# A relative-bias table stored once and read with rows shifted by one, and a delta-rule head whose instructions stand in another order

## The chip, the cores and the metric

One Trainium2 chip, one of its cores. The metric is the device time of one execution of the whole program, in microseconds (us); shorter is better.

## What is computed

Two blocks of two layers each, on 256 positions of width 1024, all in float32. The first block's layer is a feed-forward part (SwiGLU), a hybrid mixer, and a second feed-forward part. The second block's layer is a mixer with four branches and a feed-forward part. The change touches two places: the chunked delta rule of the first block's mixer, and the relative-position bias of one attention branch of the second block.

```python
# first block, mixer: for each of 8 heads and each chunk
g = cumsum(g)                                   # log decays
decay = exp(where(lower_incl, g_i - g_j, -inf))
lmat  = where(strict, (k_beta @ k.T) * decay, 0)
sol   = triangular_solve(lmat + I, [v * beta, k_beta * exp(g)])
attn_intra = (q @ k.T) * decay
...                                             # a scan over chunks gives o_a
merged = sigmoid(gate_a) * (o_a @ w_branch_a) + sigmoid(gate_b) * (o_b @ w_branch_b)
...
# second block, branch A: scores get a bias by distance
rel_idx = clip(query - key, -128, 128) + 128
scores  = q @ k.T * d**-0.5 + rel_table[:, rel_idx]
```

## The kernel before

Every weight matrix is cut into units of 128 x 2048 elements (1 MB). SyncE loads a unit into one of three slots (`load_unit`, line 242); ScalarE rounds it to a high part (`split_hi`, L248), VectorE takes the low part by subtraction (`split_lo`, L254), and TensorE multiplies with both (`product3`, L262 to L264, three matmuls for one product). A product over one unit (`feature_product`) is 48 such matmuls of 256 columns. The next load into a slot waits until the slot's unit has been split. The order of work on every engine is written out by hand; the engines meet at counting semaphores, and an engine that waits holds up all that stands behind the wait in its own list.

**The bias table.** During the first feed-forward part of layer 0, `setup_act` (L428 to L437) stores the table of relative biases to a DRAM tensor `bias_rows`: its 8 rows (2 layers x 4 heads) of 384 numbers are each written 128 times (L436), on ScalarE's DMA queue. Both layers of the second block read it back (L1532) with a row stride of 383, so that partition s gets the row that begins at 128 - s. `scores_a` (L1546) adds it to the scores by a matmul with the identity. GpSimd masks one corner (L2062).

**The mixer and its delta head.** `mix1_pe`, `mix1_act`, `mix1_dve` and `mix1_pool` first go through 28 input units (`N1`), numbered 0 to 27. The result of a "q", "k", "v" or "z" unit passes a SiLU that is made of four ScalarE operations (L809, L811, L813, L855), one VectorE operation (L916) and one GpSimd operation (L1427), one unit behind the products. The last unit, 27, is "v" heads 6 and 7. Behind the input units comes the delta head, for four groups of two heads and two chunks (`GROUPS`, the buffers `Ab`, `Mb`, `Lb`, `Ub`, `Tb`):

- TensorE (`mix1_delta_pe`): for each group four matmuls that spread the decays (`g_rows`, L1165) and four of k with k (`kk`, L1169); then for each group k with q (`qk`, L1176), which waits for `x_abs` and `glast_kept` of the group; the product of the first gate unit (28, `pair_gate_pe(0)`); a gather of the 16 x 16 diagonal blocks (L1182), which waits for the last `m_ready` and the first `attn_done`; the branch unit 29; the gate unit 30; the scatter of the inverted blocks (L1193); the branch unit 31; a product with the identity (L1200); and then three levels that merge the blocks (L1206, L1211, L1217).
- ScalarE (`mix1_delta_act`): for each group exponentials of the decays (L1279), absolute differences (L1283), the decay (L1286) and a small exponential (L1288) that waits for VectorE's `glast_kept`. Then the split of unit 31, three operations of the gate's sigmoid (L888, L890, L892), the copy of the gathered blocks (L1292) and the sigmoid's last operation (L896).
- VectorE (`mix1_delta_dve`): `glast_kept` (L1356), then L = kk x beta x decay for each group (L1364), the split of unit 31, the attention of each group (L1371), the gate's minimum (L984), and the solution of all 16 x 16 blocks, 14 dependent steps (`blocks_dve`, L1332 to L1342) with a spread behind it (L1346).
- GpSimd (`mix1_pool`): masks of the decay (L1430) and of L (L1436, it signals `m_ready`), then the decayed q (L1442).

Of the kernel before, what the change touches and what calls it, by code (L numbers as in the profile page):

```python
# [34 lines left out]
ARENA = 19712  # L35
# [45 lines left out]
def constants_2():  # L81
# [7 lines left out]
    for n in range(64, 80):  # L89
# [6 lines left out]
             "turn": turn, "freq": freq}  # L96
# [11 lines left out]
def hybrid_stack_kernel(nc, d, out):  # L108
    ctx = ExitStack()
    with ctx:  # L110
# [46 lines left out]
        bias_rows = nc.dram_tensor("bias_rows", [DEPTH, 4, P, 384], F32, kind="Internal").ap()  # L157
# [270 lines left out]
        def setup_act(e):  # L428
# [7 lines left out]
            e.dma_start(bias_rows.rearrange("l h s m -> (l h) s m"), ext.unsqueeze(1).to_broadcast([DEPTH * 4, P, 384]))\  # L436
             .then_inc(stored, 16)  # L437
# [232 lines left out]
        def b4(i):  # L670
            return bank[i][:].rearrange("p (i n) -> p i n", i=4)
# [66 lines left out]
        def pair_gate_pe(e, l, r0, u0, n):  # L738
            if n < 2:
                e.wait_ge(*V["l_done"](l, 2 * n))  # L740
            elif n < 4:
                e.wait_ge(*V["od_r"](l, 2 * n - 4))
            else:
                e.wait_ge(*V["p_scaled"](l, n - 2))
            feature_product(e, unit(r0, u0 + N1 + 2 * n), gate_bank(n), xhi, xlo)

        def pair_branch_pe(e, l, r0, u0, n):
            if n < 2:
                e.wait_ge(*V["l_done"](l, 2 * n + 1))
            elif n < 4:  # L750
                e.wait_ge(*V["od_r"](l, 2 * n - 3))
            if n == 0:
                e.wait_ge(*V["o_lo"](l, HEADS - 1))
# [31 lines left out]

        def mix1_act(e, l, r0, u0, j):
# [6 lines left out]
            for n in range(N1 + TAIL):  # L793
# [7 lines left out]
                if n - 1 in SILU:  # L801
                    m = SILU.index(n - 1)
                    if n - 1 in CONV:
                        e.wait_ge(*V["tap"](l, CONV.index(n - 1) * 4 + 3))
                    else:
                        e.wait_ge(*V["kept"](l, PLAIN.index(n - 1)))
                    if m >= 2:
                        e.wait_ge(*V["silu"](l, m - 2))
                    e.activation(sg[m % 2], home(n - 1), ACT.Abs).then_inc(V["s_abs"].sem, 1)  # L809
                    e.wait_ge(*V["s_abs"](l, m))  # L810
                    e.activation(sg[m % 2], sg[m % 2], ACT.Exp, scale=-1.0).then_inc(V["s_exp"].sem, 1)  # L811
                    e.wait_ge(*V["s_exp"](l, m))
                    e.activation(sg[m % 2], sg[m % 2], ACT.Ln, bias=one).then_inc(V["s_ln"].sem, 1)  # L813
# [38 lines left out]
                if n - 1 in SILU:  # L852
                    m = SILU.index(n - 1)
                    e.wait_ge(*V["s_min"](l, m))
                    e.activation(sg[m % 2], sg[m % 2], ACT.Exp).then_inc(V["s_sigmoid"].sem, 1)  # L855
# [48 lines left out]
        def mix1_dve(e, l, r0, u0, j):  # L904
# [3 lines left out]
            for n in range(N1 + TAIL):  # L908
# [4 lines left out]
                if n - 1 in SILU:  # L913
# [1403 lines left out]
```

## Time and profile before

| what | value |
|---|---|
| median of 3 runs | 2628.71 us (2627.85 to 2634.68) |
| profiled execution, its own time | 2631.52 us |
| its span, first to last instruction | 2629.8 us |
| TensorE matmul busy | 2460.1 us (94% of the span) |
| VectorE busy | 1531.4 us (58%) |
| ScalarE busy | 1380.6 us (52%) |
| GpSimd busy | 177.5 us (7%) |
| mean granted TensorE clock | 0.975 of full speed |
| weights and the rest read from HBM | 382.95 MB, 147 GB/s over the span |

The profiled execution's time is 1.7 us over its span and 2.8 us over the median. PE is TensorE, DVE VectorE, ACT ScalarE, POOL GpSimd, SP SyncE; L262 is line 262 of the kernel. A granted clock of 1.0 is 2.4 GHz and one of 0.5 is 1.2 GHz. Busy TensorE time includes matmuls at the lower clock, so that the share of 94% does not say that nothing can be gained there. A row of a window view has, in this order: the stretch, its length, the busy us (and instructions) of PE, PE's weight loads, DVE, ACT and POOL, the granted clock, the mean busy share of the core's 16 DMA engines, and GB/s.

### The profile page before, as it was taken

To read this page: it belongs to the slowest core of one execution; us is meant where nothing else is said; L and a number is where in the kernel's file an instruction comes from. 1 tells how busy PE (TensorE), PEld (TensorE's weight loads), DVE (VectorE), ACT (ScalarE), POOL (GpSimd) and SP (SyncE) were. 2 spreads that over 40 slices of the span, in tenths; PEclk is the share of its full clock that TensorE was granted. 3 is DMA by queue.
4 is the path that set the end of the run, shared out by engine and by line. 5 is a ranking of instruction groups with operands and counts; after the bars stand their busy time and mean duration, and the time that the engine had idled before them with its cause. 6 is when DMAs were issued, how large, how long until landed. Compare 5 with 4: busy or idle time off the path is not lost.

```text
span 2629.8 us, 42657 instructions
## 1 busy us (share of the span) xinstructions
PE 2460.1 (94%) x17457; PEld 2291.8 (87%) x17457; DVE 1531.4 (58%) x1826; ACT 1380.6 (52%) x1828; POOL 177.5 (7%) x197
## 2 busy tenths in 40 slices
PE   7996998899999999999899899999889999997998
PEld 7995988898998998898799899888879988896897
DVE  5554667555555555566655555566475555757554
ACT  5553777255544554678535555445644444555443
POOL 0000112100000000011200000000030000003000
PEclk9998999899999999999899999999989999998999
DMA  6555444125455455444314455543345554334453
GB/s 216 183 182 130 145 135 138 36 81 189 146 190 177 158 191 167 149 134 129 97 49 146 146 188 191 168 135 112 121 130 177 183 185 144 113 113 160 144 184 128
DMA packets 313127, 387.38 MB, mean 147 GB/s; under 512 B 10780, under 2 KB 288296, under 8 KB 313000
## 3 DMA queue, kind: packets, MB, share of 16 engines
q1 hardware_dynamic: 311704, 383.94, 45.7%
q10 hardware_dynamic: 1296, 1.66, 0.5%
q8 instruction: 91, 1.49, 0.2%
q14 instruction: 36, 0.29, 0.0%
HBM read 382.95 MB, written 2.62 MB: 147 GB/s over the span
## 4 chain that ended last, share of the span: by engine, by line
PE 74%; DVE 10%; ACT 9%; issue 4%; DMA 2%; POOL 0%; SPq 0%; DVEq 0%; ACTq 0%; POOLq 0%
PE bank L262 22%; PE bank L263 21%; PE bank L264 21%; DVE wlo L254 4%; ACT whi L248 4%; DVE arena L952 1%; DMA raw<-in_w_in 1%; PE bank L1211 1%; PE bank L1206 1%; PE bank L348 1%; PE bank L722 1%; DVE arena L1976 1%; ACT arena L1875 1%; ACT arena L314 1%; PE bank L1217 1%
## 5 line engine op out<-in xcount | busy, mean ns | idle before, releaser
L254 DVE TENSOR_TENSOR wlo<-raw,whi 128x2048 fp32r<-128x2048 f32 x360 | 830.3, 2307 | 525.6 <-ACT whi L248 524.6
L262 PE MATMUL bank<-xhi,whi 128*128 128x256 f32 x3712 | 1065.2, 287 | 12.1 <-DVE arena L550 6.8
L263 PE MATMUL bank<-xlo,whi 128*128 128x256 f32 x3712 | 1053.3, 284 | 0.0
L264 PE MATMUL bank<-xhi,wlo 128*128 128x256 f32 x3712 | 1053.1, 284 | 0.0
L248 ACT ACTIVATE whi<-raw 128x2048 fp32r<-128x2048 f32 x360 | 682.1, 1904 | 154.9 <-PE bank L264 133.7
L262 PEld LDWEIGHTS bank<-xhi,whi 128*128 128x128 f32 x3712 | 715.4, 193 | 23.0 <-issue 17.1
L263 PEld LDWEIGHTS bank<-xlo,whi 128*128 128x128 f32 x3712 | 715.2, 193 | 4.9 <-issue 1.9
L264 PEld LDWEIGHTS bank<-xhi,wlo 128*128 128x128 f32 x3712 | 714.9, 193 | 0.0
L262 PE MATMUL bank<-whi,yhi 128*128 128x512 f32 x608 | 238.0, 391 | 9.2 <-ACT yhi L472 6.2
L263 PE MATMUL bank<-wlo,yhi 128*128 128x512 f32 x608 | 237.4, 390 | 0.0
L264 PE MATMUL bank<-whi,ylo 128*128 128x512 f32 x608 | 236.6, 389 | 0.0
L262 PEld LDWEIGHTS bank<-whi,yhi 128*128 128x128 f32 x608 | 114.4, 188 | 33.2 <-ACT yhi L472 7.8
L264 PEld LDWEIGHTS bank<-whi,ylo 128*128 128x128 f32 x608 | 114.2, 188 | 24.6
L263 PEld LDWEIGHTS bank<-wlo,yhi 128*128 128x128 f32 x608 | 114.4, 188 | 20.9
L262 PE MATMUL bank<-yhi,whi 128*128 128x256 f32 x384 | 112.9, 294 | 13.8 <-DVE ylo L2009 12.5
L262 PE MATMUL bank<-whi,xhi 128*128 128x256 f32 (+1 forms) x320 | 107.0, 334 | 16.1 <-DVE arena L2051 11.2
L472 ACT ACTIVATE yhi<-arena 128x512 fp32r<-128x512 f32 x44 | 27.8, 632 | 167.5 <-PE bank L264 154.9
L263 PE MATMUL bank<-ylo,whi 128*128 128x256 f32 x384 | 111.7, 291 | 0.0
L264 PE MATMUL bank<-yhi,wlo 128*128 128x256 f32 x384 | 111.6, 291 | 0.0
L263 PE MATMUL bank<-wlo,xhi 128*128 128x256 f32 (+1 forms) x320 | 105.7, 330 | 0.0
L264 PE MATMUL bank<-whi,xlo 128*128 128x256 f32 (+1 forms) x320 | 105.6, 330 | 0.0
L1427 POOL TENSOR_TENSOR arena<-arena 128x512 f32<-128x512 f32 x32 | 42.4, 1324 | 931.4 <-ACT arena L855 931.4
(377 smaller groups left out, 2867.4 us busy)
## 6 DMA issues: line engine op xcount, KB each, us to landing
raw<-in_w_in SPq DMA_DIRECT2D x92, 1024.0 KB, 5.2
raw<-in_ffn_w_in SPq DMA_DIRECT2D x88, 1024.0 KB, 5.1
raw<-in_ffn_w_out SPq DMA_DIRECT2D x44, 1024.0 KB, 4.9
raw<-in_w_gate SPq DMA_DIRECT2D x32, 1024.0 KB, 5.4
raw<-in_w_up SPq DMA_DIRECT2D x32, 1024.0 KB, 5.5
raw<-in_w_down SPq DMA_DIRECT2D x32, 1024.0 KB, 5.0
raw<-in_w_branch_b SPq DMA_DIRECT2D x8, 1024.0 KB, 5.0
raw<-in_w_branch_a SPq DMA_DIRECT2D x8, 1024.0 KB, 5.0
```

The lines of the kernel that those rows point to most:

```text
L248: e.activation(whi[s][:], raw[s][:], ACT.Copy).then_inc(hi_done[s], 1)
L254: e.tensor_tensor(wlo[s][:], raw[s][:], whi[s][:].bitcast(F32), ALU.subtract).then_inc(lo_done[s], 1)
L262: e.matmul(o, ahi, bhi, start=start, stop=False, skip_group_check=True)
L263: e.matmul(o, ahi, blo, start=False, stop=False, skip_group_check=True)
L264: return e.matmul(o, alo, bhi, start=False, stop=stop, skip_group_check=True)
L314: e.activation(xn[:, t, :], x[:, t, :], ACT.Square, accum_out=sumsq[:, t:t + 1]).then_inc(sumsq_done, 1)
L348: mm = e.transpose(tp[c // 2][:, c % 2, t * P:(t + 1) * P], xn[:, t, c * P:(c + 1) * P], ident)
L472: e.activation(hhi.rearrange("p c t -> p (c t)"), hbuf, ACT.Copy).then_inc(hhi_done, 1)
L722: e.matmul(bank[2 + m % 2][:], ones, sqr[m % 2], start=True, stop=True).then_inc(V["square_sum"].sem, 1)
L952: ins = e.scalar_tensor_tensor(o, src, w, o, ALU.mult, ALU.add)
L1206: mm = e.matmul(b4(g)[:, i, :], Lb[g][:, i, :], Ub[g][:, i, :], start=True, stop=True)
L1427: e.tensor_tensor(home(n - 1), home(n - 1), sg[m % 2], ALU.mult).then_inc(V["silu"].sem, 1)
```

## The change

The bias table is now written once, 8 rows of 384 numbers. It is read with a row stride of one (`bias_by_row`), so that partition s gets the row that begins at 1 + s, which is the old partition 127 - s. The matmul that adds it uses an anti-identity (`flip`, one more constant of 128 columns in the second table) in place of the identity, and the masked corner is in partitions 0 to 63.

In the delta head nothing is added and nothing left out; the instructions stand in another order on TensorE, ScalarE, VectorE and GpSimd, and some waits are placed elsewhere.

```diff
-        bias_rows = nc.dram_tensor("bias_rows", [DEPTH, 4, P, 384], F32, kind="Internal").ap()
+        bias_rows = nc.dram_tensor("bias_rows", [DEPTH * 4, 384], F32, kind="Internal")
+        def bias_by_row(l):
+            return bass.AP(tensor=bias_rows, offset=l * 4 * 384 + 1, ap=[[1, P], [384, 4], [1, T]])
...
-            e.dma_start(bias_rows.rearrange("l h s m -> (l h) s m"), ext.unsqueeze(1).to_broadcast([DEPTH * 4, P, 384]))\
-             .then_inc(stored, 16)
+            e.dma_start(bias_rows.ap(), ext).then_inc(stored, 16)
...
-            e.dma_start(bias_a, bias_rows[l].rearrange("h s m -> h (s m)")[:, P:P + P * 383]
-                        .rearrange("h (s m) -> s h m", m=383)[:, :, 0:T]).then_inc(small_in, 16)
+            e.dma_start(bias_a, bias_by_row(l)).then_inc(small_in, 16)
...
-            e.matmul(o[:, 0:128], bias_a[:, h, 0:P], ident, start=False, stop=True, skip_group_check=True)
+            e.matmul(o[:, 0:128], bias_a[:, h, 0:P], flip, start=False, stop=True, skip_group_check=True)
...
+        KK_ORDER = (1, 2, 3, 0)
+        def place(g):
+            return KK_ORDER.index(g)
         def mix1_delta_pe(e, l, r0, u0):
             e.wait_ge(*V["o_lo"](l, HEADS - 1))
-            e.wait_ge(*V["normed"](l, len(NORM) - 1))
-            e.wait_ge(*V["pre_copied"](l, len(CONV) - 1))
-            for g in range(GROUPS):
+            for g in range(GROUPS):
+                if g < 2:
+                    e.wait_ge(*V["pre_copied"](l, len(CONV) - 2 + g))
                 for i in range(4):
                     mm = e.matmul(b4(g)[:, i, :], tile_col(gg, g, i).to_broadcast([P, P]), le, start=True, stop=True)
                 mm.then_inc(V["g_rows"].sem, 1)
-                for i in range(4):
-                    h, t = 2 * g + i // 2, i % 2 * P
-                    mm = e.matmul(b4(4 + g)[:, i, :], kT[:, h, t:t + P], kT[:, h, t:t + P], start=True, stop=True)
-                mm.then_inc(V["kk"].sem, 1)
+            pair_gate_pe(e, l, r0, u0, 0)
+            e.wait_ge(*V["normed"](l, len(NORM) - 1))
+            for g in KK_ORDER[:3]:
+                kk_pe(e, g)
             for g in range(GROUPS):
...
                 mm.then_inc(V["qk"].sem, 1)
-            pair_gate_pe(e, l, r0, u0, 0)
+            e.wait_ge(*V["p_min"](l, 0))
+            kk_pe(e, 0)
+            pair_branch_pe(e, l, r0, u0, 0)
             e.wait_ge(*V["m_ready"](l, GROUPS - 1))
             e.wait_ge(*V["attn_done"](l, 0))
...
             mm.then_inc(V["gathered"].sem, 1)
-            pair_branch_pe(e, l, r0, u0, 0)
             pair_gate_pe(e, l, r0, u0, 1)
+            pair_branch_pe(e, l, r0, u0, 1)
             for b in range(4):
...
                 mm.then_inc(V["scattered"].sem, 1)
-            pair_branch_pe(e, l, r0, u0, 1)
...
         def mix1_delta_act(e, l, r0, u0):
...
+            pair_gate_act(e, l, r0, u0, 0)
             split_hi(e, unit(r0, u0 + N1 + 3))
-            pair_gate_act(e, l, r0, u0, 0)
+            pair_sigmoid_act(e, l, 0)
+            silu_log_act(e, l, N1 - 1)
+            silu_exp_act(e, l, N1 - 1)
             e.wait_ge(*V["gathered"](l))
             e.activation(small_l, bank[0][:, 0:256], ACT.Copy).then_inc(V["l_compact"].sem, 1)
-            pair_sigmoid_act(e, l, 0)
...
-            for g in range(GROUPS):
-                e.wait_ge(*V["kk"](l, g))
+            for g in KK_ORDER:
+                if g == 0:
+                    silu_min_dve(e, l, N1 - 1)
+                e.wait_ge(*V["kk"](l, place(g)))
...
                 up.then_inc(V["l_done"].sem, 1)
+                if g == 1:
+                    pair_min_dve(e, l, 0)
+                if g == 3:
+                    attn_dve(e, l, range(3))
+            attn_dve(e, l, range(3, 4))
             split_lo(e, unit(r0, u0 + N1 + 3))
-            for g in range(GROUPS):
-                e.wait_ge(*V["a_mask"](l, g))
-                e.wait_ge(*V["qk"](l, g))
-                e.tensor_tensor(flat(Ab[g]), bank[g][:], flat(Ab[g]), ALU.mult).then_inc(V["attn_done"].sem, 1)
-            pair_min_dve(e, l, 0)
             blocks_dve(e, l)
```

`silu_log_act`, `silu_exp_act`, `silu_min_dve` and `silu_pool` are the SiLU of a unit as functions; for unit 27 they are called in the delta head. `kk_pe` and `attn_dve` are the loops that stood in place. GpSimd masks L in the order 1, 2, 3, 0 and multiplies unit 27's SiLU behind that. The spread in `blocks_dve` waits for that SiLU as well.

How the lists move is seen at three places. On **TensorE**, in the delta head of layer 0, before. The names are buffers: `table,small` spreads the decays, `arena 128x128` is kk or qk, `xhi,whi` opens a gate product, `yhi,whi` a branch product, and `128x16` is the gather.

```order
L1165 MATMUL bank<-table,small 128x128 x4
L1169 MATMUL bank<-arena 128x128 x4
...
L1176 MATMUL bank<-arena 128x128 x16
L262 MATMUL bank<-xhi,whi 128x256
...
L1182 MATMUL bank<-table,arena 128x16 x16
L262 MATMUL bank<-yhi,whi 128x256
...
L1193 MATMUL bank<-table,arena 128x128 x16
L262 MATMUL bank<-yhi,whi 128x256
```

And the same place after the change, where L1190 is the spread of the decays, L1175 kk, L1201 qk, L1209 the gather, L1220 the scatter and L1226 the product with the identity:

```order
L1190 MATMUL bank<-table,small 128x128 x16
...
L268 MATMUL bank<-xhi,wlo 128x256
L1175 MATMUL bank<-arena 128x128 x12
L1201 MATMUL bank<-arena 128x128 x16
L1175 MATMUL bank<-arena 128x128 x4
L266 MATMUL bank<-yhi,whi 128x256
...
L1209 MATMUL bank<-table,arena 128x16 x16
L266 MATMUL bank<-xhi,whi 128x256
...
L1220 MATMUL bank<-table,arena 128x128 x16
L1226 MATMUL bank<-table,arena 128x128 x16
```

The first gate product moved ahead of kk and qk, the first branch product ahead of the gather, and both products of the second pair stand between gather and scatter; nothing stands between scatter and the product with the identity.

On **VectorE**, from the last input unit's split to the blocks, before:

```order
L254 TENSOR_TENSOR wlo<-raw,whi 128x2048
L916 SCALAR_TENSOR_TENSOR arena<-arena 128x512
L1356 TENSOR_TENSOR small<-bank,small 128x1 x8
L1364 SCALAR_TENSOR_TENSOR arena<-bank,small,arena 128x128 x16
L254 TENSOR_TENSOR wlo<-raw,whi 128x2048
L1371 TENSOR_TENSOR arena<-bank,arena 128x512 x4
L984 SCALAR_TENSOR_TENSOR pre<-bank,pre 128x2x256
L1332 TENSOR_TENSOR arena<-table,arena 128x256
```

and after, with L1391 for `glast_kept`, L1401 for L, L998 for the gate's minimum, L1360 for the attention and L809 for the SiLU's minimum:

```order
L258 TENSOR_TENSOR wlo<-raw,whi 128x2048
L1391 TENSOR_TENSOR small<-bank,small 128x1 x8
L1401 SCALAR_TENSOR_TENSOR arena<-bank,small,arena 128x128 x4
L998 SCALAR_TENSOR_TENSOR pre<-bank,pre 128x2x256
L1401 SCALAR_TENSOR_TENSOR arena<-bank,small,arena 128x128 x8
L1360 TENSOR_TENSOR arena<-bank,arena 128x512 x3
L809 SCALAR_TENSOR_TENSOR arena<-arena 128x512
L1401 SCALAR_TENSOR_TENSOR arena<-bank,small,arena 128x128 x4
L1360 TENSOR_TENSOR arena<-bank,arena 128x512
L258 TENSOR_TENSOR wlo<-raw,whi 128x2048
L1366 TENSOR_TENSOR arena<-table,arena 128x256
```

The gate's minimum stands behind the first group's L, and the SiLU's minimum and the split of unit 31 came down past three groups.

On **ScalarE**, behind the last of the four groups, after the change (L905, L907, L909 and L913 are the gate's sigmoid, L795 to L804 the SiLU of unit 27, L1321 the copy of the gathered blocks):

```order
L1314 ACTIVATE small<-small 128x2
L905 ACTIVATE pre<-bank 128x2x256
L907 ACTIVATE pre<-pre 128x2x256
L909 ACTIVATE pre<-pre,const_cols 128x2x256
L252 ACTIVATE whi<-raw 128x2048
L913 ACTIVATE pre<-pre 128x2x256
L795 ACTIVATE arena<-arena 128x512
L797 ACTIVATE arena<-arena 128x512
L799 ACTIVATE arena<-arena,const_cols 128x512
L804 ACTIVATE arena<-arena 128x512
L1321 ACTIVATE arena<-bank 128x256
```

The SiLU of unit 27 stood ahead of the four groups before; now it stands behind the gate's sigmoid.

## Rows read from the trace of the kernel before

**Rows 1.** The page's chain that ended last, shares of the span by engine
```profile
PE 74%; DVE 10%; ACT 9%; issue 4%; DMA 2%; POOL 0%; SPq 0%; DVEq 0%; ACTq 0%; POOLq 0%
```

**Rows 2.** TensorE's waits over the whole span: us in total, times, longest
```profile
PE bank L1176 <- DVE small L1356: 10.5, 8, 2.3
...
PE bank L1182 <- DVE arena L1371: 10.2, 2, 5.1
...
PE bank L1165 <- ACT pre L825: 4.8, 2, 2.4
```

**Rows 3.** Windows of the same work in layer 0 and in layer 1 (columns as told above)
```profile
187.18:234.16 46.98, 24.38 (x150) 21.75 (x149) 16.54 (x16) 17.58 (x24) 0.00 (x0) 0.79 0.63 144
...
1027.93:1057.43 29.50, 24.38 (x150) 21.75 (x149) 16.54 (x16) 13.78 (x19) 0.00 (x0) 0.94 0.55 176
```

**Rows 4.** ScalarE in order of time, layer 0: start, us, instruction, [idle before, releaser]
```profile
189.22 0.80 ACTq L436 DMA_DIRECT2D bias_rows<-arena  x1
...
223.70 1.91 ACT L248 ACTIVATE whi<-raw 128x2048 fp32r<-128x2048 f32 x1 [17.77 <-DMA raw<-in_w_in]
```

**Rows 5.** The chain of waits at that place, and the page's loads of the same kind
```profile
195.35 28.33 DMA raw<-in_w_in
...
raw<-in_w_in SPq DMA_DIRECT2D x92, 1024.0 KB, 5.2
```

**Rows 6.** Window in which only the bias write is under way
```profile
214.00:216.00 2.00, 0.00 (x0) 0.00 (x0) 0.00 (x0) 0.00 (x0) 0.00 (x0) 0.54 0.52 79
```

**Rows 7.** Windows, layer 0's delta head, and its last product before L1200
```profile
444.92:506.24 61.32, 48.56 (x354) 47.78 (x354) 33.21 (x80) 27.61 (x56) 15.53 (x14) 0.89 0.22 69
...
500.40:506.24 5.84, 5.84 (x52) 5.84 (x51) 0.65 (x2) 2.92 (x3) 0.00 (x0) 1.00 0.20 64
```

**Rows 8.** Windows of the two stretches at half the clock in it
```profile
463.70:466.80 3.10, 3.10 (x16) 3.10 (x16) 3.10 (x14) 0.00 (x0) 3.10 (x3) 0.51 0.00 0
...
477.40:487.20 9.80, 9.80 (x47) 9.80 (x47) 4.13 (x15) 0.91 (x2) 0.00 (x0) 0.50 0.33 107
```

**Rows 9.** ScalarE in order of time, layer 0's delta head
```profile
447.99 1.89 ACT L248 ACTIVATE whi<-raw 128x2048 fp32r<-128x2048 f32 x1
...
455.09 0.42 ACT L1279 ACTIVATE arena<-bank 128x128 f32<-128x128 f32 x2
...
457.21 0.42 ACT L1279 ACTIVATE arena<-bank 128x128 f32<-128x128 f32 x2
...
473.71 0.58 ACT L888 ACTIVATE pre<-bank 128x512 f32<-128x512 f32 x1
...
474.99 0.72 ACT L892 ACTIVATE pre<-pre,const_cols 128x512 f32<-128x512 f32 x1
```

**Rows 10.** VectorE in order of time, layer 0's delta head
```profile
451.63 2.29 DVE L254 TENSOR_TENSOR wlo<-raw,whi 128x2048 fp32r<-128x2048 f32 x1
...
463.17 4.23 DVE L1364 SCALAR_TENSOR_TENSOR arena<-bank,small,arena 128x128 f32<-128x128 f32 x16
...
476.05 2.48 DVE L1371 TENSOR_TENSOR arena<-bank,arena 128x512 f32<-128x512 f32 x4
...
484.42 0.43 DVE L1332 TENSOR_TENSOR arena<-table,arena 128x256 f32<-128x256 f32 x1 [5.29 <-ACT arena L1292]
...
491.49 2.50 DVE L1346 TENSOR_TENSOR arena<-arena,table 128x512 f32<-128x512 f32 x4
```

**Rows 11.** GpSimd in order of time, layer 0's delta head
```profile
464.86 5.03 POOL L1436 TENSOR_TENSOR arena<-arena,table 128x512 f32<-128x512 f32 x4
```

**Rows 12.** The chain of waits: the gather, and 16 matmuls at full clock
```profile
476.88 7.08 PE bank L1182 x32
...
497.07 3.57 PE bank L1193 x32
```

**Rows 13.** DMA issues: count, KB each, us to landing
```profile
arena<-bias_rows SPq DMA_DIRECT2D x2, 512.0 KB, 6.6
...
arena<-in_g_final SPq DMA_DIRECT2D x1, 512.0 KB, 3.7
```

More of the change, by code:

```diff
@@ L738, in pair_gate_pe @@
         def pair_gate_pe(e, l, r0, u0, n):
-            if n < 2:
-                e.wait_ge(*V["l_done"](l, 2 * n))
-            elif n < 4:
+            if n == 1:
+                e.wait_ge(*V["l_done"](l, place(2)))
+            elif 2 <= n < 4:
                 e.wait_ge(*V["od_r"](l, 2 * n - 4))
-            else:
+            elif n >= 4:
                 e.wait_ge(*V["p_scaled"](l, n - 2))
@@ L748, in pair_branch_pe @@
             if n < 2:
[L749 removed]
+                e.wait_ge(*V["l_done"](l, place(2 * n + 1)))
             elif n < 4:
                 e.wait_ge(*V["od_r"](l, 2 * n - 3))
[L752 to L753 removed]
             if n == 4:
@@ L784, in home, with silu_log_act, silu_exp_act, silu_min_dve @@
             return HOME[KINDS.index(kind)][:, 2 * g:2 * g + 2, :].rearrange("p h t -> p (h t)")
+        def silu_log_act(e, l, n):
+            m = SILU.index(n)
+            if n in CONV:
+                e.wait_ge(*V["tap"](l, CONV.index(n) * 4 + 3))
+            else:
+                e.wait_ge(*V["kept"](l, PLAIN.index(n)))
+            if m >= 2:
+                e.wait_ge(*V["silu"](l, m - 2))
+            e.activation(sg[m % 2], home(n), ACT.Abs).then_inc(V["s_abs"].sem, 1)
+            e.wait_ge(*V["s_abs"](l, m))
+            e.activation(sg[m % 2], sg[m % 2], ACT.Exp, scale=-1.0).then_inc(V["s_exp"].sem, 1)
+            e.wait_ge(*V["s_exp"](l, m))
+            e.activation(sg[m % 2], sg[m % 2], ACT.Ln, bias=one).then_inc(V["s_ln"].sem, 1)
+        def silu_exp_act(e, l, n):
+            m = SILU.index(n)
+            e.wait_ge(*V["s_min"](l, m))
+            e.activation(sg[m % 2], sg[m % 2], ACT.Exp).then_inc(V["s_sigmoid"].sem, 1)
+        def silu_min_dve(e, l, n):
+            m = SILU.index(n)
+            e.wait_ge(*V["s_ln"](l, m))
+            e.scalar_tensor_tensor(sg[m % 2], home(n), 0.0, sg[m % 2], ALU.min, ALU.subtract).then_inc(V["s_min"].sem, 1)
+        def silu_pool(e, l, n):
+            m = SILU.index(n)
+            e.wait_ge(*V["s_sigmoid"](l, m))
+            e.tensor_tensor(home(n), home(n), sg[m % 2], ALU.mult).then_inc(V["silu"].sem, 1)
         def mix1_act(e, l, r0, u0, j):
@@ L800, in mix1_act @@
                     stick_softplus_act(e, l, head_at(n, 1))
[L801 to L813, printed above, removed]
+                if n - 1 in SILU and n < N1:
+                    silu_log_act(e, l, n - 1)
                 if head_at(n, 3) is not None:
@@ L1326, in mix1_delta_act, with attn_dve @@
                 e.activation(flat(Tb[g]), flat(Tb[g]), ACT.Exp, scale=-0.5).then_inc(V["od_r"].sem, 1)
+        def attn_dve(e, l, which):
+            for g in which:
+                e.wait_ge(*V["a_mask"](l, g))
+                e.wait_ge(*V["qk"](l, g))
+                e.tensor_tensor(flat(Ab[g]), bank[g][:], flat(Ab[g]), ALU.mult).then_inc(V["attn_done"].sem, 1)
         def blocks_dve(e, l):
@@ L1431, in mix1_pool @@
                  .then_inc(V["a_mask"].sem, 1)
-            for g in range(GROUPS):
-                e.wait_ge(*V["l_done"](l, g))
+            for g in KK_ORDER:
+                e.wait_ge(*V["l_done"](l, place(g)))
                 e.wait_ge(*V["a_mask"](l, g))
```

40 lines of the change are left out of this document (20 added, 20 removed).

## The prediction, made before the change was run

> **What bounds the kernel now.** First the page's chain of work that ended last: three quarters of it is TensorE [rows 1]. So time is gained only where TensorE waits or runs at the lower clock. Next TensorE's waits. Three of them lie in the delta head, in both layers: 2.4 us for the last unit's copy, 5.3 us ahead of the four qk groups, 5.1 us ahead of the gather; 12.8 us in each layer [rows 2]. Third, windows of the same work in the two layers, from VectorE's last operation on block 9 of the first feed-forward part to the mixer's first normalised chunk. TensorE is busy 24.38 us in both, yet layer 0 takes 46.98 us and layer 1 takes 29.50 us [rows 3]: 17.5 us that only layer 0 pays. Fourth, the granted clock in the delta head: 0.89 on average over 61.32 us [rows 7], and two stretches of 3.1 and 9.8 us at the 1.2 GHz level [rows 8].
>
> **Part 1: the bias table.** The write of the old table, 1536 KB, is issued at 189.22 us. After it ScalarE waits 17.77 us for a load of weights, until 223.70 us [rows 4]. The load had been issued at 195.35 and landed 28.33 us later, where its kind takes 5.2 us [rows 5]. In 214 to 216 us, where TensorE, VectorE and ScalarE all stand still, half of the DMA engines are busy and move 79 GB/s [rows 6]: the write, which the load shares its engines with. The new write has one 128th of the bytes. The load then lands at about 200.6 us; ScalarE wants it at 205.9 (223.70 less 17.77). So 5 us of cover remain, and layer 0 costs here what layer 1 costs, which has no such write: **-17.5 us** [rows 3].
>
> The Trainium skill speaks against this part (DMA: Bandwidth & Descriptors, Specifications): its fabric ceiling of 435 GB/s would move 1.57 MB in 3.6 us, an estimate from that page. By it the write would be over long before the load is wanted, and part 1 would be worth nothing. The row at 79 GB/s decides; what the rule gives is the third rival.
>
> Reading is unchanged in size: 512 KB, 6.6 us to landing [rows 13]. That 128 partitions now read over the same few KB has a neighbour in the trace: the final gain, 512 KB read from one row of 4 KB, lands in 3.7 us [rows 13]. I price it at nothing; its cover is the four input units that are multiplied before the table is needed. The matmul with the other constant has the same shape. The constant adds 64 KB to one load that is issued two units ahead: nothing.
>
> **Part 2: the delta head.** I take layer 0's times; layer 1's waits are the same. The end that counts is the product with the identity (L1200), which starts at 506.24. A product over one unit takes 5.8 us [rows 7], 16 square matmuls 3.6 us at full clock [rows 12], four of them 0.9. Step by step, with TensorE:
>
> 1. It frees at 444.9. The first group's spread of decays needs no wait any more, but the second group's still needs the copy at 447.2: 1.5 us of the 2.4 us wait stays. The spreads end at 450.0.
> 2. The gate product, which stood behind qk, follows: to 455.8. Three groups of kk: to 458.5.
> 3. ScalarE. The SiLU of unit 27 no longer stands ahead of the groups, so they begin when the split at 447.99 ends, at 449.8 instead of 455.09 [rows 9]. Group 0 waits for VectorE, whose split ends at 453.9 [rows 10], until 454.1. The next three follow at the pitch of 2.12 us (457.21 less 455.09), to 460.6. That hides the stalls between qk groups; qk runs through to 462.1.
> 4. The gate's three operations take 2.0 us (473.71 to 475.71 [rows 9]), to 462.7, and its minimum on VectorE 0.7, to 463.4. TensorE waits 1.3 us for it (new wait), then kk of group 0 to 464.4 and the branch product to 470.2.
> 5. On VectorE two groups of L at 1.06 (4.23 over 4), three attentions at 0.62 (2.48 over 4) [rows 10], the SiLU's minimum at 0.7 and L of group 0 end at 469.1; ScalarE's SiLU, behind a split of 1.9, delivers at 467.2, in time. GpSimd's last mask takes 1.26 (5.03 over 4 [rows 11]), to 470.4. The gather starts at 470.5, not 476.88. The split of unit 31 comes down past all this and ends at 471.9; its product needs it at 479.8.
> 6. The gather is 32 array operations of 7.08 us, all at half clock [rows 8, 12]. At full clock I take 3.6 us, since as many operations of the scatter take 3.57 [rows 12]; it is the same number of weight loads. The two ends are 3.6 and 7.1. It ends at 474.1.
> 7. Two products: to 485.6. Under them the blocks, 7.07 us from 484.42 to 491.49, and the spread of 2.5 [rows 10] end on VectorE at 484.1, 1.5 us before they are wanted. The spread also waits for unit 27's SiLU, which GpSimd has done by 471.8. Scatter to 489.2.
> 8. The last copy of the scatter's result on ScalarE was hidden by a branch product; now TensorE waits 0.7 us for it. VectorE's share (a scaling, a split of 2.3, a minimum and two copies behind the spread) ends at 489.0, only just in time.
>
> L1200 starts at 489.9: **-16.3 us in each layer**. As a cross-check, waits fall from 12.8 to 3.8 (1.5, 1.3, 0.3, 0.7), which is 9.0; the clock gives back up to 11% of 61.3, which is 6.7 [rows 7]. That is 15.7, and 0.6 of rounding at the joints. Behind L1200 the order is unchanged and the loads have been issued earlier, not later.
>
> The sum is 17.5 + 2 x 16.3 = 50.1 us off the profiled execution's 2631.5: 2581.4. That execution lies 2.8 over the median of the runs, so I give 2578.6, rounded to **2579 us**.
>
> **The clock, and what I do not know.** The clock fell at 463.7 behind a stretch whose waits were all short, the longest 2.4 us, and at 477.4 behind 5.1 us of waiting. It did not come back in the gather (476.88 to 483.96 [rows 12]) but only under the branch product behind it, at 487.2 [rows 8]. [...] The Trainium skill (TensorE: Matmul & The Clock Gate, "Why this matters for your kernels") names idle gaps as what takes the clock down. By that the gather would cost nothing more; the first fall speaks against reading it so narrowly.
>
> **Rivals.**
> - *The clock falls again* in or behind the gather. For: it stayed low through the gather. Against: it is granted in full through all the later levels with their small matmuls, and the gather is now half as long. Price from 1 to 7.3 us a layer (16.3 less 9.0, all of the clock's share): 2581 to 2593 us.
> - *The wait moves to VectorE or GpSimd.* Steps 5, 7 and 8 have covers of 0 to 1.5 us. Each late us costs one: about 2 a layer, 2583 us.
> - *The write is worth nothing*, since the load is late for another reason. Against it speaks layer 1. 2628.7 less 32.6 is 2596 us.
> - *Slower than before:* 128 rows from one spot of DRAM are read one after the other. The write moved 79 GB/s on eight engines, 10 on each; a read that falls to one engine's 10 GB/s takes 52 us in place of 6.6, 45 more in each layer. Less the 50 gained that is 2628.7 + 91 - 50 = 2670 us. It decides from 25 us more per read on. The final gain's 3.7 us speaks against it.
> - *The order changes nothing*, as the head is bound by its chain of data on all engines, and only the write counts: 2611 us. The 5 us that ScalarE's groups come forward speak against it.
>
> **How the numbers follow.** Chances: my forecast 0.62, the clock 0.2, the moved wait 0.1, the write worth nothing 0.02, only the write 0.03, slower 0.02, and 0.01 that nothing is seen. The range goes from 2574 (2 us in each layer for the roundings of eight steps) to 2592 (nearly all of the clock's share lost in both layers). A difference under 0.3%, some 8 us, can't be told from none. Faster 0.97, same 0.01, slower 0.02.
>
> **What would show it.** Layer 0's window from rows 3 at about 29.5 us, and no load of 28 us in the chain. The delta head from the last input product to the product with the identity at 45 us in place of 61.3, with waits of TensorE of about 4 us; the wait for p_min above 1 us and one of 0.7 ahead of L1226. The gather at 3.6 us. A gather of 7 us, or a clock of 0.5 behind it, is the first rival; a wait on VectorE or GpSimd ahead of the gather or scatter the second. I am wrong as a whole if layer 0 still waits for that load, or if the product with the identity comes less than 9 us earlier.

## The result, and the profile after

The change runs in 2593.07 us (median of 4, 2591.27 to 2595.65), beside 2630.2 us for the kernel before on the same chip (2627.85 to 2634.68): a ratio of 0.9858, 95% interval 0.9841 to 0.9875. That is 37 us faster where 50 were forecast, and 1 us above the top of the range. The profiled execution took 2591.27 us (span 2589.5, mean clock 0.98).

The page of the change, its chain that ended last, by engine:

```profile
PE 75%; DVE 10%; ACT 9%; issue 4%; DMA 0%; POOL 0%; SPq 0%; DVEq 0%; ACTq 0%; POOLq 0%
```

The 2% of DMA of [rows 1] are gone. The waits of TensorE, the ones that answer to [rows 2] (total us, times, longest):

```profile
PE bank L1190 <- ACT pre L844: 2.8, 2, 1.4
...
PE bank L1175 <- DVE pre L998: 2.3, 2, 1.1
...
PE bank L1226 <- ACT arena L1326: 1.6, 2, 0.8
```

L1190 is the spread of the decays, L1175 kk and L1226 the product with the identity. The gather (L1209) is not in the list. It waits 0.3 us a layer for GpSimd's last mask, as the first row of weight loads below shows; before, it waited 5.1 us.

Windows of the change: layer 0's stretch of [rows 3], the whole delta head (from the last input product to L1226, as in [rows 7]), the gather, the stretch from the fall of the clock into the gate product, and the gate product:

```profile
186.02:215.50 29.48, 24.36 (x150) 21.73 (x149) 16.44 (x16) 17.64 (x24) 0.00 (x0) 0.93 0.54 178
425.39:475.21 49.82, 46.40 (x354) 45.66 (x352) 34.03 (x80) 25.27 (x55) 19.47 (x14) 0.93 0.26 85
450.79:457.90 7.11, 7.11 (x33) 7.11 (x34) 2.09 (x1) 0.00 (x0) 6.00 (x5) 0.73 0.45 147
454.00:461.60 7.60, 7.60 (x39) 7.60 (x40) 2.80 (x13) 2.18 (x2) 2.79 (x5) 0.55 0.42 137
457.74:465.09 7.35, 7.35 (x51) 7.35 (x52) 5.81 (x28) 2.18 (x2) 0.00 (x0) 0.79 0.00 0
```

Layer 0's stretch is now as long as layer 1's was: 17.5 us are gone. The head takes 49.8 us in place of 61.3; 45.0 were forecast. In it the gather takes 7.1 us again, and the gate product behind it 7.35 us, at a mean clock of 0.79; with the full clock it takes 6.0 (e4 below).

ScalarE of the change where the write is issued. It needs 0.28 us, and the splits follow with no wait for a load (in [rows 4] ScalarE waited 17.77 us):

```profile
188.12 0.28 ACTq L440 DMA_DIRECT2D bias_rows<-arena  x1
...
202.93 3.71 ACT L252 ACTIVATE whi<-raw 128x2048 fp32r<-128x2048 f32 x2
```

The change's DMA issues answer to [rows 13]. The read of overlapping rows costs what the old one did:

```profile
arena<-bias_rows SPq DMA_DIRECT2D x2, 512.0 KB, 6.6
arena<-in_g_final SPq DMA_DIRECT2D x1, 512.0 KB, 3.6
```

The chain of waits through the end of the head (start us, us, what), where [rows 12] stood before:

```profile
449.44 1.30 POOL arena L1471
450.79 7.12 PE bank L1209 x32
457.90 0.40 PE bank L266
...
470.86 3.59 PE bank L1220 x32
474.46 0.61 ACT arena L1326
475.21 3.81 PE bank L1226 x32
```

Gather, scatter and product with the identity are 32 array operations each; the first takes twice as long as the others. Its weight loads, in the change and for comparison L1226's (count, busy us, mean ns, idle before):

```profile
L1209 PEld LDWEIGHTS bank<-table,arena 128*128 128x128 f32 x64 | 14.0, 310 | 0.6 <-POOL arena L1471 0.6
...
L1226 PEld LDWEIGHTS bank<-table,arena 128*128 128x128 f32 x64 | 7.3, 192 | 1.9 <-issue 1.9
```

A weight load of the gather takes 310 ns where a 128 x 128 load of L1226, at the full clock, takes 192 ns. The gather's weights are `M_blocks[:, :, c]`, every 16th float32 of a row of 2048, a step of 64 bytes. That set the theories for the experiments. **A**: the step makes the gather slow, and the clock falls in or behind it because each of its matmuls multiplies only 16 columns (its moving operand). **B**: the gather is slow because the clock falls in it, as I had read it in the kernel before.

### The profile page after: what moved, and what is told of

Its sections match the earlier page's. It is cut to its first block, busy times and chain, and to the rows that moved or that the text cites. A ratio compares the mean times of both kernels' runs of the same rounds, so it can differ in the third digit from the quotient of the medians.

```text
span 2589.5 us, 42657 instructions
## 1 busy us (share of the span) xinstructions
PE 2457.9 (95%) x17457; PEld 2289.9 (88%) x17457; DVE 1532.7 (59%) x1826; ACT 1380.5 (53%) x1828; POOL 185.5 (7%) x197
## 4 chain that ended last, share of the span: by engine, by line
PE 75%; DVE 10%; ACT 9%; issue 4%; DMA 0%; POOL 0%; SPq 0%; DVEq 0%; ACTq 0%; POOLq 0%
PE bank L266 22%; PE bank L267 21%; PE bank L268 21%; DVE wlo L258 4%; ACT whi L252 4%; DVE arena L966 1%; PE bank L1237 1%; PE bank L1232 1%; PE bank L352 1%; PE bank L725 1%; DVE arena L2011 1%; ACT arena L1910 1%; ACT arena L318 1%; PE bank L1243 1%; PE bank L1209 1%
```

## The experiments

### The two parts alone

```diff
 # e1_bias_only: the kernel before, with
+            e.dma_start(bias_rows.ap(), ext).then_inc(stored, 16)
+            e.dma_start(bias_a, bias_by_row(l)).then_inc(small_in, 16)
 # (and flip, and the other masked corner); head and all else as before
 # e2_head_only: the change, with
-            e.dma_start(bias_rows.ap(), ext).then_inc(stored, 16)
+            e.dma_start(bias_rows.rearrange("l h s m -> (l h) s m"), ext.unsqueeze(1).to_broadcast([DEPTH * 4, P, 384]))\
+             .then_inc(stored, 16)
 # (and the old read, ident, the old corner)
```

> The kernel before with the bias table of the change alone (written once, read with a stride of one row element, anti-identity); the delta head stands as before. If the write of 1.5 MB was what held the load back: layer 0's window from VectorE's last operation on block 9 to the first normalised chunk falls from 47.0 to about 29.5 us and the time falls by 17 to 19 us, to about 2612; the delta head stays at 61.3 us. Rival (the load was late for another reason): the window stays near 47 us and the time near 2630.

> The changed kernel with the old bias table put back; the delta head in its new order. If the two parts add: the time falls by what is left of the change's 37 us, 19 to 22 us, to about 2609, the head from the last input product to the product with the identity takes 49.8 us in both layers as in the change, and layer 0 keeps its wait of 17.8 us for the load. Rival (the parts share something, for instance the phase of the clock): the two parts' gains sum to less than 33 or to more than 41 us.

Measured: the table alone 2612.95 us (2611.49 to 2614.1), ratio 0.9938 [0.9922, 0.9955]; the head alone 2610.25 us (2606.98 to 2611.16), 0.9926 [0.9909, 0.9942]; beside them the kernel before took 2629.61. So 16.7 and 19.4 us, together 36.0, where both at once brought 37. The parts add, within 1.1 us. The table is worth what was forecast, within 1 us. The head is worth 19 in place of 33: that is where the shortfall lies. In the profile of the head alone, the head takes 49.9 us in both layers, as in the change within 0.1.

In the profile of the table alone, the stretch of [rows 3] is as short as in the change:

```profile
186.02:215.50 29.48, 24.33 (x151) 21.72 (x151) 16.45 (x16) 18.09 (x24) 0.00 (x0) 0.95 0.56 178
```

### The gather: the step of its weights, and its width

```diff
 # e3_gather_unstrided
-  mm = e.matmul(bank[0][:, c * BLK:(c + 1) * BLK], M_blocks[:, :, c], const("row_of"), start=True, stop=True)
+  mm = e.matmul(bank[0][:, c * BLK:(c + 1) * BLK], arena[:, 10240 + c * P:10240 + (c + 1) * P], const("row_of"), start=True, stop=True)
 # e4_gather_wide
-  mm = e.matmul(bank[0][:, c * BLK:(c + 1) * BLK], M_blocks[:, :, c], const("row_of"), start=True, stop=True)
+  mm = e.matmul(bank[0][:, c % 4 * P:(c % 4 + 1) * P], M_blocks[:, :, c], ident, start=True, stop=True)
```

> The changed kernel, but the 16 matmuls of the gather take 128 neighbouring columns as weights in place of every sixteenth one; the blocks that it solves are therefore not those of L. Theory (the weights' stride of 16 elements makes the weight loads slow): the gather falls from 7.1 to 3.6 us at the full clock, each layer gains 3.5 us and perhaps the 1.5 us of the clock behind it as well: 7 to 10 us below the change. Rival 1 (128x16 matmuls are slow because they are narrow): the gather stays at 7.1 us and the time at that of the change. Rival 2 (it was the clock alone): the same, 7.1 us.

> The changed kernel, but the gather multiplies with the identity of 128 columns in place of 16 columns, with the same strided weights; what it writes is not the blocks of L. Theory (weights' stride sets the gather's 7.1 us; its few columns take the clock down): the gather still takes 7.1 us, the granted clock stays at 1.0 through it and through the gate product behind it, which falls from 7.35 to 5.9 us: 1.5 us a layer, about 3 us below the change. Rival (the clock falls for the slow weight loads or for the waits ahead, whatever the columns): the clock falls again at the same place and the time is that of the change within 1 us.

Neither gathers the diagonal blocks: the first multiplies neighbouring columns in place of them, the second transposes slices with the identity. Measured: 2585.5 us (2583.26 to 2587.68) and 2590.99 us (2590.46 to 2595.35). The gather in the chain of waits, first without the step, then with it and 128 columns:

```profile
450.49 4.17 PE bank L1209 x32
```

```profile
450.90 7.25 PE bank L1209 x32
```

In the first, part of the gather ran at the half clock (mean 0.87).

Windows of the second, the gather and the gate product behind it:

```profile
450.90:458.16 7.26, 7.26 (x34) 7.26 (x35) 2.09 (x1) 0.00 (x0) 5.98 (x5) 1.00 0.46 144
457.91:463.91 6.00, 6.00 (x52) 6.00 (x52) 4.58 (x22) 2.18 (x2) 0.00 (x0) 1.00 0.00 0
```

Here the clock is at its full 2.4 GHz all through and the gather still takes 7.26 us. That excludes theory B: without any fall of the clock the step gives the whole length. The gather's loads take the same in the change, where the clock falls at 454.0 in the middle of it, as here at the full clock. First the change, then this run:

```profile
L1209 PEld LDWEIGHTS bank<-table,arena x64: 291/310/312, 450.8 to 1269.8; 128*128 128x128 f32 x64
```

```profile
L1209 PEld LDWEIGHTS bank<-table,arena x64: 291/312/313, 450.9 to 1267.0; 128*128 128x128 f32 x64
```

The three numbers are the smallest, median and largest ns. What happens to the clock goes with the width: with 16 columns it falls in or behind the gather, with 128 it holds, and the gate product takes 6.0 us. The profiles of all runs in the new order agree. In the 3 us behind the gather the granted clock is 0.50 to 0.58 in all 13 layers with 16 columns, and 1.00 in all 7 with 128.

### The same computation with another layout

The masked L is written so that the gather finds the weights of one column side by side. GpSimd writes with the step in place of TensorE reading with it:

```diff
 # e5_gather_layout
-        M_blocks = arena[:, 10240:12288].rearrange("p (b c) -> p b c", c=BLK)
+        M_columns = arena[:, 16384:18432].rearrange("p (c b) -> p c b", c=BLK)
...
-                e.tensor_tensor(Mb[g], Lb[g], const("below").unsqueeze(1).to_broadcast([P, 4, P]), ALU.mult)\
+                o = M_columns[:, :, g * 32:g * 32 + 32].rearrange("p c (i k) -> p i k c", i=4)
+                e.tensor_tensor(o, src, below, ALU.mult).then_inc(V["m_ready"].sem, 1)
...
-                mm = e.matmul(bank[0][:, c * BLK:(c + 1) * BLK], M_blocks[:, :, c], const("row_of"), start=True, stop=True)
+                mm = e.matmul(bank[0][:, c * BLK:(c + 1) * BLK], M_columns[:, c, :], const("row_of"), start=True, stop=True)
 # e6_layout_wide: as e5, and the 16 columns eight times
+                mm = e.matmul(bank[0][:, c * BLK:c * BLK + P], M_columns[:, c, :],
+                              const("row_of").unsqueeze(1).to_broadcast([P, P // BLK, BLK]), start=True, stop=True)
```

> The changed kernel, with GpSimd writing its masked L column by column (stride 128) into the free buffers behind it, so that each of the gather's 16 matmuls reads 128 neighbouring weights; nothing is left out. Theory: the gather takes 3.6 us in place of 7.1, and since its 16 columns still take the clock down, the product behind it stays slow for some 3 us: the time of the run with neighbouring weights, about 2586, 7 us below the change. If GpSimd's strided writes are slower than its 1.27 us for a group, the last of them delays the gather by as much, up to 1 us a layer. Rival (the earlier run gained by something else than the stride): within 2 us of the change.

> As the one before, and each matmul of the gather multiplies with its 16 columns repeated eight times (128 columns, of which the next matmul overwrites all but the first 16). Nothing is left out. Theory (width holds the clock, stride sets the length; the two are independent): the gather takes 3.6 us, the granted clock stays at 1.0 through it and behind it, the product behind it takes 5.9 us, and the head from the last input product to the product with the identity takes 49.8 less 3.5 less 1.5, about 45 us, which is what the prediction had: about 2583, 10 us below the change. Rival (the clock also falls for the short waits ahead of the gather): as the one before, about 2586.

> The change itself again, for a second profile. Theory on the 1.5 us that each layer gave back behind the head (a fall of the clock at the 2.4 us wait ahead of the output product, which the kernel before also has, without the fall): the fall comes and goes from one execution to the next, so this profile has it in some of the four output products of the first block's layers and not in the same ones. Rival (the new order causes it): both layers have it again. The time is 2593 within 3 us either way.

Measured, beside 2630.08 us for the kernel before: the layout 2585.91 us (2584.5 to 2587.01), 0.9832 [0.9818, 0.9845]; the layout with 128 columns 2589.29 us (2587.62 to 2591.47), 0.9846 [0.9833, 0.986]; the change again 2591.89 us (2589.46 to 2593.45), 0.9853 [0.9838, 0.9868]. The layout is the fastest version found that does the whole computation (e8 below, at 2587.07 us, is too near to tell apart), and no run of it was as slow as the fastest of the change. GpSimd's mask takes no longer for that: 1.31 us in place of 1.30. The second profile of the change was to settle whether a fall of the clock that both layers have at the 2.4 us wait ahead of the output product, and that the kernel before has not, comes and goes. It does not: both layers have it again, so it comes with the new order. The windows behind that wait, layers 0 and 1:

```profile
603.20:606.30 3.10, 3.10 (x8) 2.42 (x8) 3.01 (x4) 1.47 (x1) 0.00 (x0) 0.50 0.72 252
1415.50:1418.50 3.00, 3.00 (x8) 2.32 (x9) 2.91 (x4) 1.62 (x1) 0.00 (x0) 0.50 0.81 284
```

In the chain of the layout version:

```profile
450.61 1.31 POOL arena L1474
451.97 3.75 PE bank L1209 x32
...
468.82 3.59 PE bank L1220 x32
472.43 0.61 ACT arena L1326
...
473.17 3.81 PE bank L1226 x32
```

The four heads side by side, the row of each from its own profile: the change's 49.82 stands above. With the step and 128 columns (e4):

```profile
425.49:474.02 48.53, 45.09 (x353) 44.34 (x352) 33.88 (x80) 25.25 (x55) 19.45 (x14) 1.00 0.24 77
```

without it and with 16 columns (e5):

```profile
426.57:473.17 46.60, 43.17 (x352) 42.42 (x352) 34.99 (x80) 25.25 (x55) 19.66 (x14) 0.96 0.26 84
```

and without it, with 128 columns (e10, the second profile of e6's kernel):

```profile
427.12:472.44 45.32, 41.67 (x353) 40.90 (x351) 34.96 (x80) 25.46 (x55) 19.71 (x14) 1.00 0.23 74
```

The step costs 3.2 us at either width (49.82 less 46.60, 48.53 less 45.32), the narrow columns 1.3 us with either layout. Without both the head takes 45.3 us; the forecast was 45.0.

### Why the shortest head does not give the shortest kernel

That last version has the shortest head and takes 3.4 us more than the layout with 16 columns. I cut each profile at the ten additions of rows that end each part, and give the length of each stretch:

| us | layer 0: FFN, then mixer | FFN | FFN | layer 1: mixer | FFN | 2nd block: mixer | FFN | mixer | FFN |
|---|---|---|---|---|---|---|---|---|---|
| before | 227.85, 424.86 | 199.38 | 199.03 | 424.15 | 199.40 | 281.25 | 191.18 | 280.83 | 188.54 |
| change | 209.27, 414.03 | 199.20 | 199.03 | 414.13 | 199.19 | 281.12 | 191.17 | 280.59 | 188.59 |
| e5, layout | 207.72, 413.61 | 199.25 | 199.03 | 410.91 | 199.15 | 281.09 | 191.17 | 280.56 | 188.59 |
| e6, layout, wide | 207.74, 409.66 | 200.98 | 201.43 | 409.87 | 200.97 | 281.10 | 191.06 | 282.67 | 188.77 |

FFN is a feed-forward part. The code of the feed-forward parts and of the second block is the same in all. Yet in e6 two of the feed-forward parts take 1.7 and 1.8 us more than in e5 and one 2.4, and a mixer of the second block 2.1. So I asked whether that is chance, or follows from the head:

```diff
 # e8_wide_in_first: as e6, and
+                if l:
+                    mm = e.matmul(bank[0][:, c * BLK:(c + 1) * BLK], M_columns[:, c, :], const("row_of"), start=True, stop=True)
+                    continue
 # e9_layout_again is e5, e10_layout_wide_again is e6
```

> The gather reads neighbouring weights in both layers, and multiplies 128 columns in layer 0 and 16 in layer 1. Between the adds of rows at the end of layer 0's mixer and at the end of the next one (numbers 1 and 3 of ten), the version with 128 columns in both layers took 402.4 us, with 16 in both 398.3 us; layer 0's mixer itself took 409.7 and 413.6 us. Theory A, a wait that comes later brings a fall of the clock or none according to what TensorE did before it, so that a fall avoided in the head comes back at the unchanged waits behind it: layer 0's half as with 128 columns in both (409.7 and 402.4 us), layer 1's mixer and what follows as with 16 in both (410.9, 199.2 and 280.6 us), 2586 us in all. Theory B, the extra falls of that version lie in its own instructions or are chance from one execution to the next: the stretches behind layer 0's mixer take 398.3 us, and it runs in 2582 us.

> The version with neighbouring weights and 16 columns once more, for a second profile. Theory A (falls follow from the order of the work): the same stretches as in its first profile within 0.5 us: layer 0's mixer 413.6 us to 1 us, the two behind it 199.2 and 199.0 us, layer 1's mixer 410.9 us, then 199.2, 281.1, 191.2 and 280.6 us; 2586 us. Theory B (chance): some stretch differs by 1.7 to 2 us.

> The version with neighbouring weights and 128 columns once more. Theory A: the stretches of its first profile again, 409.7 us for layer 0's mixer, 201.0 and 201.4 behind it, 409.9 for layer 1's mixer, then 201.0, 281.1, 191.1 and 282.7 us; 2589 us. Theory B: two or more of the three stretches that were 1.8 to 2.4 us above those with 16 columns fall back to 199.2, 199.0, 199.2 or 280.6 us.

| us | layer 0: FFN, then mixer | FFN | FFN | layer 1: mixer | FFN | 2nd block: mixer | FFN | mixer | FFN |
|---|---|---|---|---|---|---|---|---|---|
| e9, as e5 | 209.42, 411.16 | 199.23 | 199.05 | 410.86 | 199.14 | 281.13 | 191.17 | 280.45 | 188.62 |
| e10, as e6 | 210.09, 410.55 | 198.69 | 201.01 | 409.71 | 201.00 | 280.91 | 191.04 | 282.68 | 188.76 |
| e8 | 209.19, 410.54 | 198.69 | 201.01 | 410.89 | 199.15 | 281.10 | 191.18 | 280.56 | 188.59 |

Medians: e8 2587.07 us (2585.59 to 2588.51), e9 2586.75, e10 2589.85, the kernel before 2630.62. Both theories were half right. From layer 1's mixer on, the stretches repeat within 0.2 us by the width in that layer: 128 columns always 409.8 and then 201.0 and 282.7, 16 columns always 410.9, 199.15 and 280.5. The other profiles in the new order, e4 with 128 columns, and the change, e2, e3 and e7 with 16, have the same two stretches behind the mixer, within 0.1 us. There the price follows from the head: 1.1 us won in the mixer, 1.8 and 2.1 lost behind it. In layer 0 chance has its part: the same kernel took 413.61 and 411.16 us in its mixer (e5, e9), and 200.98 and 198.69 us in the part behind it (e6, e10); the 402.4 us for the two parts behind it did not come back in e8 and e10, which took 399.7.

What the added 1.8 us are is seen at a wait that both have. In layer 1 TensorE waits 1.9 us ahead of 1452.5 in both profiles; windows of the 3.4 us behind that wait, and of the 5.4 us behind the wait of 3.7 us at the start of the next mixer, in e5:

```profile
1452.64:1456.00 3.36, 3.36 (x28) 3.36 (x29) 1.59 (x2) 2.33 (x2) 0.00 (x0) 1.00 0.89 305
1633.63:1639.00 5.37, 4.45 (x25) 3.85 (x26) 2.85 (x7) 3.57 (x13) 0.00 (x0) 0.72 0.31 97
```

and in e10:

```profile
1452.52:1456.00 3.48, 3.48 (x17) 3.48 (x18) 1.72 (x2) 2.33 (x2) 0.00 (x0) 0.55 0.85 294
1635.02:1640.50 5.48, 4.83 (x22) 3.98 (x23) 2.96 (x7) 3.68 (x13) 0.00 (x0) 0.50 0.27 85
```

At the first wait the clock is 1.00 behind it in one and 0.55 in the other; 28 matmuls begin in the one window and 17 in the other. At the second the clock is low for longer in e10, but that mixer is no longer for it (281.1 and 280.9 us). The 2.1 us in the last mixer are time at the lower clock too. TensorE's waits there add up to 19.3 us in e5 and 19.1 in e10, and its busy time is 2.3 us longer in e10:

```profile
2101.93:2382.49 280.56, 261.39 (x1860) 238.55 (x1859) 178.71 (x268) 147.71 (x237) 37.31 (x28) 0.96 0.42 131
```

```profile
2103.00:2385.68 282.68, 263.68 (x1860) 239.54 (x1859) 178.76 (x267) 147.71 (x237) 37.30 (x28) 0.96 0.41 130
```

The mean clock is the same 0.96; in e10 more of the low clock lies over work and less over waits. So a fall costs nothing to 2 us, by what it covers, and removing one ahead changed the later ones. What decides for a given wait, no run here shows.

## Why the prediction was wrong, and where it was right

**Part 1, the table: right.** 17.5 us forecast, 17.5 in the window, 16.7 by the run with it alone. The load no longer waits, the read stays at 6.6 us. One reading was wrong. [rows 6] is called a window in which only the bias write is under way, and the prediction gives it all of the 79 GB/s. But the load issued at 195.35 is under way there too. The DMA view of 214 to 216 us by queue (packets, MB, share of the 16 engines), first the queue of the write and then that of the loads:

```profile
q10 hardware_dynamic: 63, 0.10, 43.9%
q1 hardware_dynamic: 60, 0.06, 8.6%
```

So the write moved some 50 GB/s and the load some 30, where 1 MB in 5.2 us [rows 5] is some 200. That fits a load held back on engines that it shares; the 17.5 us do not rest on the 79. The Trainium skill's ceiling of 435 GB/s (DMA: Bandwidth & Descriptors, Specifications) would, by the prediction's estimate, have made it worth nothing; the run of the table alone excludes that. The rival of a read from one spot (2670 us, priced from the same 79 GB/s) is out, as the read lands in 6.6 us.

**Part 2, by its steps**, in us from the end of the last input product:

| step | forecast | the change |
|---|---|---|
| 1, spreads end | 5.1 | 5.2 |
| 2, gate product ends | 10.9 | 11.0 |
| 3, qk ends | 17.2 | 17.3 |
| 4, wait for the minimum | 1.3 | 1.15 |
| 5, gather starts | 25.6 | 25.4 |
| **6, gather** | **3.6** | **7.1** |
| 7, two products | 11.5 | 13.0 |
| 8, wait ahead of L1226 | 0.7 | 0.8 |
| L1226 starts | 45.0 | 49.8 |

Seven of the eight steps hold: six within 0.3 us, and step 7 but for the clock, which fell to half over its first 3 us. The ScalarE rows of the change show it: the first group, the next two and the gate's first operation, forecast (19.5 us earlier than in the prediction, as the head begins that much earlier) for 430.3, 434.6, 436.7 and 441.1:

```profile
430.26 0.43 ACT L1305 ACTIVATE arena<-bank 128x128 f32<-128x128 f32 x2
...
434.66 0.43 ACT L1305 ACTIVATE arena<-bank 128x128 f32<-128x128 f32 x2
...
436.78 0.42 ACT L1305 ACTIVATE arena<-bank 128x128 f32<-128x128 f32 x2
...
441.02 0.58 ACT L905 ACTIVATE pre<-bank 128x512 f32<-128x512 f32 x1
```

**Step 6 failed.** I wrote "at full clock I take 3.6 us, since as many operations of the scatter take 3.57 [rows 12]; it is the same number of weight loads". The number was the same, the loads were not: the gather's have a step of 64 bytes between elements and take 310 ns, where those of neighbouring elements take 192 at the full clock. The gather took 7.1 us with the clock full for its first 3.2 us, and 7.26 us with the clock full all through (e4). That is 3.5 us in each layer. Without the step it took 3.75 us (e5).

The times of the kernel before could not tell the two causes apart. Both its gathers ran at half the clock, and there a load of neighbouring elements is no faster than one with the step. From the kernel before, a load of the gate product at half the clock and one behind it at the full clock, and then the gather's:

```profile
465.00 0.33 PEld L262 LDWEIGHTS bank<-xhi,whi 128*128 128x128 f32 x1
...
466.98 0.19 PEld L263 LDWEIGHTS bank<-xlo,whi 128*128 128x128 f32 x1
```

```profile
L1182 PEld LDWEIGHTS bank<-table,arena x64: 291/310/312, 476.9 to 1306.0; 128*128 128x128 f32 x64
```

At half the clock these products start a matmul every 0.21 us, so that 32 would take some 6.8 us without any step, an estimate from those rows. The half clock alone therefore fitted the 7.08 us [rows 8, 12], and so did the step, which stands in the code. The other end of my range, 7.1, was the value. And the sign that I gave, "a gather of 7 us" for the first rival, was none: e4 has it at the full clock. The Trainium skill says what the step does (SBUF — State Buffer, the box on cachelines under "Door 1: The DMA port swizzle"): lines are 16 bytes, and an access that goes to a new line each time pays, so that four float32 are as far as one can step for free. The trace agrees for a step of sixteen, with 310 ns for 192 at the full clock; no run here tries a shorter step.

**The first rival was right as well**, at its low end. The clock falls inside the gather, with no wait of TensorE's near, and the gate product takes 1.4 us more. The Trainium skill (TensorE: Matmul & The Clock Gate, "Why this matters for your kernels") speaks of idle gaps. Here TensorE's last wait of more than 0.3 us was the 1.15 us ahead of group 0's kk, which ended 7 us before the gather began, and with 128 columns in place of 16 and the same waits the clock held (e4). So these falls follow the 16-column gather and no gap, with the 310 ns loads and with the 192 ns loads (e5) alike. Besides, each layer pays 1.5 us for a fall at a wait that had none in either layer before. It is the wait of 2.4 us ahead of the output product; a window behind it in layer 0, before:

```profile
631.87:634.50 2.63, 2.63 (x12) 2.17 (x13) 2.53 (x4) 1.76 (x1) 0.00 (x0) 1.00 0.94 329
```

and in the change:

```profile
600.93:603.50 2.57, 2.57 (x6) 2.11 (x7) 2.48 (x4) 1.77 (x1) 0.00 (x0) 0.50 0.94 329
```

I had written that behind L1200 the order is unchanged. So it is, and the price of its waits is not. The prediction put this term at nothing. The second profile of the change has the fall in both layers again, and the profile of the table alone (e1), with the old order, has the full clock there in both (1.00). In e4's layer 0 the clock held behind this wait (granted 1.00), and its mixer kept all that its head had won: 13.3 us for 12.8.

**The sum.** Forecast 50.1 us; between the two profiled executions 40.2. Missing per layer are 3.5 (step), 1.3 (1.5 for the clock behind the gather, less 0.2 in the other steps) and 1.5 (fall at the output product); 12.6 for both. Gained are 0.8 in layer 0's mixer, 1.1 ahead of the window of [rows 3] and 0.7 in the other stretches together: 10 us short. The forecast of 2578.6 is 14.5 us under the measured median. The other 4.6 of these are the choice of executions: before's lay 2.8 above the median of three runs, which I took off, and the change's lies 1.8 under its own. With more runs the kernel before has medians of 2629.6 to 2630.6, so that 2.8 was 1 to 2 us too much.

The wait did not move to VectorE or GpSimd. Step 5's cover was thin, as said, and the gather did wait 0.3 us for GpSimd's last mask, as forecast.

## What to carry to other kernels

Before a duration is carried from one matmul to another, compare the access patterns of both operands and not only the count and shape; a low clock that lies over the same stretch can hide a second cause, as it did here, and then the trace before cannot show it. The question to ask is what the stretch would cost at the other clock. Where a few matmuls read float32 weights with a step, let the engine that writes them lay them out. A gain of 1 to 2 us from a clock that is kept is not safe until the parts behind it are measured too: the next waits can take it back.

## What the runs showed that I had not expected

- **A float32 weight load with a step of 64 bytes** takes 291 to 313 ns at either clock. One of neighbouring elements takes 192 ns at the full clock and 330 at half. 16 fp32 matmuls with the step take 7.1 to 7.3 us against 3.75 to 4.2 without it. The same step on GpSimd's write cost nothing that can be seen (1.30 and 1.31 us).
- **The falls of the clock move, and their prices repeat.** Two unchanged parts behind layer 1's mixer took 199.2 or 201.0 us, and 280.6 or 282.7, with nothing between, by the width of 16 matmuls that ended some 165 us ahead of the first of them.
- **VectorE and GpSimd held each other up** where both ran operations with two inputs in SBUF. VectorE's split took 3.12 us in place of 2.29 as it began under GpSimd's mask, and GpSimd's SiLU behind it 3.32 in place of 1.26 to 1.45. From VectorE and GpSimd of the change in order of time:

```profile
449.76 3.12 DVE L258 TENSOR_TENSOR wlo<-raw,whi 128x2048 fp32r<-128x2048 f32 x1
```

```profile
449.44 1.29 POOL L1471 TENSOR_TENSOR arena<-arena,table 128x512 f32<-128x512 f32 x1 [1.89 <-DVE arena L1401]
450.69 3.32 POOL L814 TENSOR_TENSOR arena<-arena 128x512 f32<-128x512 f32 x1
```

  The mask ends at 450.73; 2.15 us later, at 452.88, the split ends; 1.13 us later the SiLU. Each fits, within 0.2 us, an operation that stood still until the other was done; no run here varies it. The Trainium skill says so of a pair of ports that is held for a whole instruction (SBUF — State Buffer, "SBUF: two separate sides"), and the trace agrees. Nothing waited for these two here.
